# A hybrid encoder layer on one Trainium2 core: first norm and values' projection as one stage by token blocks, memory norm beside the mixer's output projection, query norm beside the memory keys

## The reference

```python
h = x
hn = _rmsnorm(h, g_mix)                      # first norm
qg, kg, vg, og, alr, qs, ks, vs = split(hn @ w_in)   # vg: "values" of gated linear attention
o_gla = _gla(...); o_sb = _stick_breaking(...)
h = h + concatenate([o_gla, o_sb]) @ w_out   # mixer's output projection
# memory cross attention: query norm of h, memory norm of the 256 memory tokens
h = h + _mem_xattn(_rmsnorm(h, g_mem_q), _rmsnorm(mem, g_mem_kv), w_mq, w_mkv, w_mo)
h = h + _peer(_rmsnorm(h, g_ffn), w_pq, sub_keys, peer_u, peer_v)   # 128 experts per token
return _rmsnorm(h, g_final)

def _rmsnorm(x, g):
    return x * rsqrt(mean(x * x, axis=-1) + 1e-6) * g
```

## Time and profile before

| | |
|---|---|
| three runs | 3676.73 us median (3675.47 to 3676.82) |
| profiled execution | 3675.01 us, span 3673.3 us |
| busy share of the span | PE 78%, DVE 69%, ACT 41%, POOL 42% |
| first norm (mixnorm), first activation table load to last low part | 2.8 to 45.9 us |
| values' projection (glavalues), first matmul to last copy | 46.6 to 94.0 us |
| mixer's output projection (mixout), first load to last squares' sum | 615.2 to 669.1 us |
| memory and query norm (memnorms) | 669.5 to 693.9 us |
| memory keys (memk), first matmul to last copy | 694.7 to 719.8 us |

### The profile page before, as it was taken

One profiled execution on the slowest core, in us unless ns is written; L12 is line 12 of the kernel. 1 busy time (PEld: TensorE's weight loads), 2 busy tenths in 40 slices (PEclk: granted clock), 3 DMA queues, 4 the chain that ended last, 5 costly groups with the idle time before them and its releaser, 6 DMA issues.

```text
span 3673.3 us, 32325 instructions
## 1 busy us (share of the span) xinstructions
PE 2882.7 (78%) x8696; PEld 1449.3 (39%) x8696; DVE 2548.4 (69%) x5651; ACT 1509.2 (41%) x3964; POOL 1525.6 (42%) x1176
## 2 busy tenths in 40 slices
PE   6998999797998788788878888767666666666666
PEld 5777544676733333343323333222222222222222
DVE  3453454443477877888778777877787787778776
ACT  3221596422233543554344433443344334434343
POOL 0000111000055555545555555555656655566654
PEclk9999999898999899989999999888899888889988
DMA  2101002212399999999999999999999999999998
GB/s 81 41 24 46 1 1 103 86 63 80 123 415 418 420 415 416 408 406 419 418 413 417 409 415 413 406 409 416 418 405 420 414 414 414 417 413 416 416 413 347
DMA packets 177619, 1156.07 MB, mean 315 GB/s; under 512 B 19984, under 2 KB 22048, under 8 KB 46240
## 3 DMA queue, kind: packets, MB, share of 16 engines
q0 software_dynamic: 147456, 1073.81, 71.1%
q1 hardware_dynamic: 29984, 80.26, 6.1%
HBM read 1149.80 MB, written 4.19 MB: 314 GB/s over the span
## 4 chain that ended last, share of the span: by engine, by line
DMA 39%; PE 11%; ACT 8%; issue 7%; DVE 5%; POOL 2%; POOLq 0%; DVEq 0%; ACTq 0%
DMA early_rows<-in_uv,choice_index 21%; DMA rows<-in_uv,choice_index 18%; PE expert_acc L2201 10%; ACT L2077 2%; ACT L1367 2%; DVE expert_own_acc L1951 2%; DVE early_rows L1975 1%; ACT expert_wt L2079 1%; POOL early_rows L1467 1%; ACT expert_dg L2088 1%; DVE rows L1975 1%; ACT expert_wt L2077 1%; POOL rows L1467 1%; ACT choice_best L1367 1%; PE expert_side L2127 0%
## 5 line engine op out<-in xcount | busy, mean ns | idle before, releaser
L2201 PE MATMUL expert_acc<-early_rows,expert_dg 128*128 128x512 f32 x1756 | 954.8, 679 | 370.6 <-ACT expert_dg L2088 367.5
L1467 POOL DMA_INDIRECT early_rows<-in_uv,choice_index x586 | 843.1, 1439 | 724.2 <-PE expert_acc L2201 393.6
L2201 PE MATMUL expert_acc<-rows,expert_dg 128*128 128x512 f32 x1316 | 733.5, 693 | 299.3 <-ACT expert_dg L2088 297.4
L1975 DVE CUSTOM_DVE_ANT_0 early_rows<-early_rows,expert_xn 128x1024 f32<-128x1024 f32 x586 | 716.8, 1223 | 319.4 <-DMA early_rows<-in_uv,choice_index 315.3
L1467 POOL DMA_INDIRECT rows<-in_uv,choice_index x438 | 632.6, 1444 | 551.2 <-PE expert_acc L2201 313.0
L2077 ACT ACTIVATE expert_wt<-expert_dot 128x1 f32<-128x1 f32 x1024 | 208.9, 204 | 1475.6 <-DVE expert_dot L1975 1474.7
L2201 PEld LDWEIGHTS expert_acc<-early_rows,expert_dg 128*128 128x128 f32 x1756 | 344.9, 211 | 937.9 <-ACT expert_dg L2088 625.9
L1975 DVE CUSTOM_DVE_ANT_0 rows<-rows,expert_xn 128x1024 f32<-128x1024 f32 x438 | 535.7, 1223 | 233.8 <-DMA rows<-in_uv,choice_index 229.0
L2201 PEld LDWEIGHTS expert_acc<-rows,expert_dg 128*128 128x128 f32 x1316 | 265.3, 216 | 736.9 <-ACT expert_dg L2088 489.8
L2088 ACT ACTIVATE expert_dg<-ident,expert_wt 128x128 f32<-128x128 f32 x768 | 309.6, 403 | 24.9
L2079 ACT ACTIVATE expert_wt<-expert_wt,choice_gate 128x1 f32<-128x1 f32 x1024 | 303.9, 297 | 33.4
(11 more groups left out here) (356 smaller groups left out, 3945.1 us busy)
## 6 DMA issues: line engine op xcount, KB each, us to landing
early_rows<-in_uv,choice_index POOLq DMA_INDIRECT x586
H<-in_x SPq DMA_DIRECT2D x8, 1024.0 KB, 10.2
pq_w_raw<-in_w_pq SPq DMA_DIRECT2D x16, 512.0 KB, 3.3
expert_w_raw<-in_w_pq SPq DMA_DIRECT2D x32, 256.0 KB
rows<-in_uv,choice_index POOLq DMA_INDIRECT x438
stick_w_raw<-in_w_feat SPq DMA_DIRECT2D x8, 512.0 KB, 3.3
tok_w_raw<-in_w_tok SPq DMA_DIRECT2D x8, 512.0 KB, 4.3
out_w_raw<-in_w_out SPq DMA_DIRECT2D x8, 512.0 KB, 6.7
```

What stands on the lines that cost most here:

```text
L1467: pool.indirect_dma_start(out=self.rows[R % self.ROWS], out_offset=None, in_=uv, in_offset=bass.IndirectOffsetOnAxis(ap=index, axis=0), bo ...
L1975: nc.vector.tensor_tensor_reduce(rows[R % ROWS][:, 0:D], rows[R % ROWS][:, 0:D], xn[:, :], 1.0, 0.0, ALU.mult, ALU.add, dot[:, h % 2, r:r ...
L2201: last_mm = nc.tensor.matmul(acc[:, h * HALF:(h + 1) * HALF], dg[:, n % DG, :], rows[R % ROWS][:, D + h * HALF:D + (h + 1) * HALF], start= ...
```

## The change

Three stages are written anew. `normed_values_phase` takes the place of the first `norm_phase` and of `glavalues`: tokens go by pairs of blocks, each pair with its own sums and roots; PE finishes one token block with all four pieces of the weight (kept whole in SBUF as high and low parts) before it goes to the next, and transposes block b + 1 before the products of block b. `mixer_out_phase` takes the place of the mixer's output projection and norms the memory tokens on the way; its weights now have two raw slots in place of four. `memory_keys_phase` takes the place of the keys' stage and norms the queries on the way. The stage `memnorms` between them is gone. The norm's steps beside other work are the methods of a class `BlocksNorm` (not shown where they are those of `norm_phase`).

```diff
+def normed_values_phase(co, xv, piece, gain, place, x, rstd, xs, w_raw, heads):
...
+            tokens(0)
+            weight(0)
+            tokens(1)
+            for j in range(1, PIECES):
+                weight(j)
+            tokens(2)
+            tokens(3)
+            co.fetch_upcoming(sp)
...
+            def weight_high(j):
+                act.wait_ge(w_landed[j], 16)
+                high(nc, w_hi[:, j, :], w_raw[:, j, :]).then_inc(w_hi_ready, 1)
...
+            square(0)
+            guess(0)
+            weight_high(0)
+            weight_high(1)
+            for p in range(PAIRS):
+                scale(2 * p)
+                scale(2 * p + 1)
+                if p + 1 < PAIRS:
+                    square(p + 1)
+                part(2 * p)
+                if p == 0:
+                    weight_high(2)
+                    weight_high(3)
+                if p + 1 < PAIRS:
+                    guess(p + 1)
+                part(2 * p + 1)
+            co.high_of_next(act)
...
+            for p in range(PAIRS):
+                take(2 * p)
+                if p + 1 < PAIRS:
+                    square(p + 1)
+                    variance(p + 1)
+                part(2 * p)
+                if p == 0:
+                    weight_low(2)
+                else:
+                    empty(2 * p - 2)
+                take(2 * p + 1)
+                if p == 0:
+                    weight_low(3)
+                if p + 1 < PAIRS:
+                    refine(p + 1)
+                part(2 * p + 1)
+                if p:
+                    empty(2 * p - 1)
...
+            turn(0)
+            turn(1)
+            for b in range(NB):
+                if 2 <= b < NB - 1:
+                    turn(b + 1)
+                for j in range(PIECES):
+                    values(b, j)
+                    if b == 1 and j == 0:
+                        turn(2)
...
+def mixer_out_phase(co, x, nb, w, add, loads, tok, m_tok, sums, gain, m_place, rstd):
...
+            for n in range(w.pre, w.n):
+                w.highs(act, n, n % U)
+                if n == 1:
+                    act.wait_ge(extra, 16 * len(loads))
+                    for b in range(MB):
+                        link(nc.scalar.activation(junk[:, :], m_tok[:, b, :], ACT.Square, accum_out=sums[:, b:b + 1]))
+                    act.sem_inc(memory_summed, 1)
+                if n == 3:
+                    norm.guess(act)
+                if n == 4:
+                    norm.scale(act, 0)
+                if n == 5:
+                    norm.high(act, 0)
+                    norm.scale(act, 1)
+                if n == 6:
+                    norm.high(act, 1)
...
+def memory_keys_phase(co, x, w, out, tok, sums, gain, place, rstd):
...
+            for n in range(w.n):
+                if 0 <= n - FIRST < nb:
+                    norm.turn(pe, n - FIRST)
+                pe.wait_ge(w.ready, n + 1)
...
+            for n in range(w.pre, w.n):
+                w.highs(act, n, n % U)
+                b = n - FIRST
+                if -1 <= b < nb - 1:
+                    norm.scale(act, b + 1)
+                if 0 <= b < nb:
+                    norm.high(act, b)
...
+                b = n - FIRST
+                if 0 <= b < nb:
+                    norm.take(dve, b)
+                if 0 <= b - 1 < nb:
+                    norm.low(dve, b - 1)
...
-            w_out = pieces("out_w", KT, NB // 2, a['w_out'], mix)
...
+            w_out = pieces("out_w", KT, NB // 2, a['w_out'], mix, raw_slots=2)
```

More of the change, by code:

```diff
@@ new lines, in memory_keys_phase, with _ @@
+def memory_keys_phase(co, x, w, out, tok, sums, gain, place, rstd):
+    nc = co.nc
+    w.begin()
+    bank_full, bank_free = w.used, co.sem("memk_bank_free")
+    U, nb, FIRST = w.U, NB // 2, 3
+    with ExitStack() as cx:
+        banks = [cx.enter_context(nc.psum_tensor(f"memk_bank{j}", [P, HALF], F32)) for j in range(U)]
+        norm = BlocksNorm(co, "qnorm", cx, tok, nb, gain, place, sums, rstd, 2)
+        block = cx.enter_context(nc.Block())
+        @block.gpsimd
+        def _(pool):
+            co.clear_stale(pool)
+        @block.sync
+        def _(sp):
+            w.loads(sp)
+            co.fetch_upcoming(sp)
+        @block.tensor
+        def _(pe):
+            pe.sem_inc(bank_full, 2)
+            for n in range(w.n):
+                if 0 <= n - FIRST < nb:
+                    norm.turn(pe, n - FIRST)
+                pe.wait_ge(w.ready, n + 1)
+                if n >= U:
+                    pe.wait_ge(bank_free, n - U + 1)
+                for k in range(KT):
+                    last = product(nc, banks[n % U][:, 0:MEM], w.operand(n, slice(k * P, (k + 1) * P)), x(k, 0),
+                                   k == 0, k == KT - 1)
+                last.then_inc(bank_full, 1)
+        @block.scalar
+        def _(act):
+            act.preload_act_table_set(LN_EXP)
+            norm.guess(act)
+            for n in range(w.pre, w.n):
[5 more added lines that the diff above has]
+                    norm.high(act, b)
+            co.high_of_next(act)
+        @block.vector
+        def _(dve):
+            norm.variance(dve)
+            norm.refine(dve)
+            for n in range(w.pre, w.n + 1):
+                if n < w.n:
+                    w.lows(dve, n, n % U)
+                else:
+                    co.low_of_next(dve)
+                if n:
+                    dve.wait_ge(bank_full, n - 1 + 2 + 1)
+                    nc.vector.tensor_copy(out(n - 1), banks[(n - 1) % U][:, 0:MEM]).then_inc(bank_free, 1)
+                b = n - FIRST
[3 more added lines that the diff above has]
+                    norm.low(dve, b - 1)
@@ L2265, in program @@
         HS = SEQ // HALF
-        kv = ctx.enter_context(ExitStack())
+        kv, kx = ctx.enter_context(ExitStack()), ctx.enter_context(ExitStack())
         with mix:
@@ L2303, in add @@
                 return nc.vector.tensor_tensor(h, h, bank[:, :], ALU.add)
-            w_out = pieces("out_w", KT, NB // 2, a['w_out'], mix)
-            tok_q = lambda b: m_tok[:, b, :] if b < MB else co.H[:, b - MB, :]
-            token_gemm_phase(co, "mixout", by_tokens(x_t), NB // 2, w_out, add, loads=loads + more, squares=(tok_q, sums_q, 0, MB))
+            w_out = pieces("out_w", KT, NB // 2, a['w_out'], mix, raw_slots=2)
+            m_t = [co.sb(f"m_t_{part}", [P, KT, MEM], F32R, ctx=kv, side="right") for part in ("hi", "lo")]
+            w_mk = pieces("mk_w", KT, 1, a['w_mk'], kx, raw_slots=2, side="right").ahead()
+            mixer_out_phase(co, by_tokens(x_t), NB // 2, w_out, add, loads + more, lambda b: co.H[:, b, :], m_tok, sums_q,
+                            gains[:, 2, :], by_block(m_t), rstd[:, 0:MB])
         z_b = co.sb("z_b", [P, KT, HALF])
@@ L2314, in program @@
                 with kv:
[L2315 to L2324, removed]
+                    w_mv = pieces("mv_w", KT, MB, a['w_mv'], kv, raw_slots=2).ahead()
+                    with kx:
+                        memory_keys_phase(co, by_half(MEM, m_t), w_mk, lambda n: k_t[:, n, :], lambda b: co.H[:, b, :],
+                                          sums_q[:, MB:MB + NB // 2], gains[:, 1, :], by_block(y_t), rstd[:, MB:MB + NB // 2])
                     w_mq = pieces("mq_w", KT, 1, a['w_mq'], kv, raw_slots=2).ahead()
```

244 lines of the change are left out of this document (236 added, 8 removed).

## The result

The changed kernel takes 3648.36 us (median of 4 runs, 3647.04 to 3649.01) against 3676.1 us for the kernel before (3674.64 to 3676.82 beside it): a ratio of 0.9924, 95% interval 0.9912 to 0.9936, or 27.7 us less. The forecast was 3652 us, 24.7 less.

The account below looks back on a forecast made before the run. From about a quarter of the span gathering bounds the kernel, untouched; the stages ahead stand in a row, so savings come off the end: -18.8 + 8.3 - 14.2 = -24.7, from 3676.7 to 3652 us, range 3645 to 3661.

Parts of the forecast that it names:

- Part 1: First norm and values: first product at 21.2 in place of 46.6, less 6.5 for transposes; -18.8 us, bounds -20 to -12.
- the same slow start: Values' products: PE's 192 products begin at the low clock as before, first products 0.43 apart, then 0.227.
- rival 2: First stage: PE waits about 1 to 1.5 us at each block's start for DVE, total 3660; chance 0.13.
- Part 2: Mixer's projection: a new wait +4.0, transposes between products +2.2, low clock +2.1; sum +8.3 us (6 to 11).
- the wait: Mixer's projection: PE idles +4.0 near weight piece 2, loaded behind 5 MB, with memory's squares ahead on ACT; 0 to +5.3.
- Part 3: Memory norm gone, keys beside the query norm: 36.5 us in place of 50.7, -14.2; bounds -23 to -10.
- The ring: Keys' stage: handovers DVE gain, ACT query high, ACT weight high, DVE weight low, DVE copy; 4.99 a tile against PE's 3.97.
- two allowances: Keys' stage: 0.4 for semaphores and 1.5 for a low clock, taking the last copy's 34.6 to 36.5.
- The 0.4 for semaphores: Keys' stage: 0.4 us added for the semaphores of eight handovers.
- the 1.5 for a low clock: Keys' stage: 1.5 us added for a low clock after PE's pause at the stage's start; bounds 0 and 2.8.
- Rival 3: Keys' stage: the clock stays low through PE's pauses, Part 3 worth about +1, total 3667; chance 0.07.
- rival 5: Gathering: it ends at the same time for another reason, so the gain is taken back, 3672 to 3680; chance 0.04.

Follow-up runs that it names:

- a_only: Changed kernel with the old stages for mixer's projection, norm and keys, so only the new first norm and values; 3657.05 us, ratio 0.9947 to the kernel before.
- b_undone: Changed kernel with the old mixer's projection and the memory tokens normed in a stage of their own before the keys; 3651.67 us, ratio 0.9933.
- sq_late: Changed kernel with ACT's memory-token squares moved from behind weight piece 1 to behind piece 3 in the mixer's projection, loads unchanged; 3646.47 us.
- mem_first: Changed kernel with memory tokens loaded ahead of the 4 MB of tokens in the mixer's projection, these behind weight piece 3; 3641.68 us, ratio 0.9903.
- after_again: The changed kernel measured once more, unaltered, on the chip of the next run; 3648.22 us (3645.69 to 3649.09).
- high_first: Changed kernel with ACT making the next weight's high part before the query block's high part in the keys' stage; 3641.88 us, ratio 0.9907.
- scale_first: Changed kernel with ACT scaling blocks 0 and 1 before the high part of weight piece 1 in the first stage; 3647.53 us.

## Why the prediction was right, step by step

The measured time lies in the range (3645 to 3661), 3.6 us below the forecast, and each of the three parts went the way and nearly the length that was worked out.

**Part 1, -20.5 for -18.8.** Shown by `a_only`. The start of the first product was right to 0.3. The term that was too small a gain is "the same slow start": before, PE ran 6.1 us at 1.2 GHz from its first product on, now 3.4. The clock was up when the first product came (it took 0.50, the length of a fast start): among the 16 transposes ahead of it the first start 0.213 apart and the last three 0.110, so they take 3.29 us against 3.67 in the earlier trace rows. That is worth 2.7 x 0.47 = 1.3, and transposes at 1.04 in place of 1.09 another 0.3. This is partly luck. The clock was up at the first product in four of the seven profiles with this first stage; in `b_undone` and `sq_late` it came up only 5.6 and 5.8 us behind the first product, as the prediction had it, and the last copy of values ended at 74.6, which is -19.4. PE never waited for DVE, so rival 2 (1 to 1.5 us a block) is out.

**Part 2, +7.6 for +8.3.** The mechanism was shown by `mem_first`, which takes it away, and divided by `sq_late`: the wait is there, its place is piece 2, and it is mostly the queue of transfers. Idle 3.8 for 4.0, transposes 2.1 for 2.2, clock 1.6 for 2.1. That each term fits so well is partly luck: the idle time is 3.8 to 5.6 in the five profiles with this order of loads and of squares, and in `after_again` the low clock takes 5.9 us of PE's work behind the pause and not 3.4, so that the part costs 7.6 to 10.0. The landing of piece 2 behind 5 MB took 13.8 to 15.1 after its issue in all profiles with this order of loads. The rule of ring order (the Trainium skill, "DMA: Bandwidth & Descriptors", section "Queues, rings and completion order"), weighed in the prediction, agrees with every one of these landings: they come in the order of the issues. The clock fell in all five profiles with a pause of 3.83 or more, and not in `sq_late`, whose pause was 3.06.

**Part 3, -16.2 for -14.2.** The ring was the bound, as `high_first` shows by removing it. Without two allowances the working ends at 34.6 from the last squares' sum, and 34.6 is what was measured; both were over-priced. The 0.4 for semaphores was not needed: the ring took 4.76, where the prediction's jobs add to 4.99 and its tiles are stepped by 4.9, since an engine's next instruction starts some 0.1 before the last one's recorded end. And the 1.5 for a low clock cost nothing: the clock was low (656.2 to 659.6), but in tile 0, behind which PE had to wait for DVE's refinement in any case. In `mem_first` and `sq_late`, where the clock was 1.00 throughout that stage, it took the same 33.96 and 33.95 us (33.96 in the changed kernel). I had counted that wait and the slow tile one after the other, where they lie side by side.

**Rival 3** (the clock stays low in the keys' stage) did not come: the granted clock was 1.00 from 660 to the end of the stage, through four pauses of 0.8 to 1.6 and four rows of transposes. So the rule of the Trainium skill that stood behind it ("TensorE: Matmul & The Clock Gate", "Part 4: PE-mode transpose": transposes do not count as activity for the clock) didn't decide anything here. The transposes of part 1 speak against it a second time: PE had run nothing else when their steps went from 0.213 to 0.110.

**What was missing**: the stage of memory values, +1.4, which I had put at nothing. Its matmuls last 392 ns in place of 389 (median of 32; 389 in `a_only` too, 392 to 395 in the ten profiles with the new keys' stage, where the memory tokens' parts lie on the other side of SBUF), and they start 0.232 apart in place of 0.227; with 96 of them that is about 0.4 of it. That the place in SBUF is the cause was not tried. The rest changes from profile to profile with the landing of a weight piece (ACT waits 2.9 for one in the changed kernel). Why these landings would come later behind the new keys' stage was not tried and is open.

The gathering took what it took: from its first product to its last 2652.4 us before, 2652.5 after, and 2652.1 to 2656.7 over all profiles. Nothing was taken back there (rival 5), and its spread of 4.6 us is the noise against which the single edits had to be read.

## What to carry to other kernels

When two stages are merged, list for each engine what stands ahead of the job that the bound engine waits for, in the order of the code, and for each queue what is ahead of the transfer: here 4 MB of tokens, all landed by 610 and first used at 627, stood in front of the memory tokens and of the half MB of weight that everybody needed, and another order of the issues gave 5.8 us in the stage. If work is put beside the bound engine, look for a ring: a job of the guest between two jobs of the host on each of two engines adds up, though either engine has room (DVE was busy 23 of 34 us). Where a slow start lies beside a wait that is counted anyway, don't count both.

## What the runs showed of the hardware that was not expected

- Transposes alone lifted TensorE's clock ahead of the first product: of the 16, in 3.29 us, the last three started 0.110 apart and the ones before 0.213, and the first product took 0.50 us. But not always: in `mem_first`, `b_undone` and `sq_late` the same 16 at the same place took 3.67 to 3.68, the first product 0.80, and the fast pace came 3.7 to 5.8 us behind it. So when the clock rises isn't a matter of how much work there was alone, and a gain of 1 us from an earlier rise is not to be counted on.
- The granted clock reads 1.00 from the start of a profile to the first change that it records, whatever the pace is: in `scale_first` it reads 1.00 from 21 to 22 us, where products start 0.427 apart, and 1.00 from 25 to 26, where they start 0.227 apart. In that first stretch the steps of the products say what the clock is, not the column.
- The clock can fall after PE has already resumed: idle from 613.45, resumed at 617.28, low from about 618.6 to 622.0. In `after_again` it fell while PE still stood (idle from 611.16, low from 615.9, resumed at 616.80) and stayed low until 622.7. So the price of such a pause differs from run to run, here 1.6 against 5.9 x 0.47 = 2.8.
